# First product of a hybrid attention layer: tokens stationary and not turned, weights held for two sweeps, another order in the last unit, rotation tables made between the rows of x

## The reference

```python
h = rmsnorm(x, norm_w)
qa, ka, va, ga, qb, kb, vb, gb = split(h @ w_in)      # 8 differential heads; 16 q heads on 2 kv heads
qa, ka, qb, kb = rope(rmsnorm(each))                  # cos and sin of position * inv_freq
oa = sum over the causal keys of (softmax(qa0 ka0) - lam * softmax(qa1 ka1)) * va, in 128-query blocks
ob = softmax([band of 256 keys, sink]) @ vb           # window 128
y  = [rmsnorm(oa) * subln_w * (1 - lam_init) * silu(ga), ob * silu(gb)]      # (1024, 2048)
out = x + y @ w_out
```

## Time and profile before

| what | us |
|---|---|
| median of 3 runs | 1784.22 (1783.39 to 1784.88) |
| the profiled execution's own time | 1783.47 |
| its span, first to last instruction | 1781.7 |
| PE busy | 1745.5 (98%) |
| PEld busy | 1470.9 (83%) |
| DVE busy | 1190.4 (67%) |
| ACT busy | 813.5 (46%) |
| POOL busy | 450.0 (25%) |
| mean granted TensorE clock | 0.997 of full |

### The profile page before, as it was taken

How to read it: one execution, slowest core, us unless ns; L and a number is a source line. 1 busy time by engine, 2 the same in 40 slices (tenths; PEclk the granted TensorE clock), 3 DMA queues, 4 the chain that set the end, 5 groups by cost and what they waited for, 6 DMA issues and landing times.

```text
span 1781.7 us, 28435 instructions
## 1 busy us (share of the span) xinstructions
PE 1745.5 (98%) x8904; PEld 1470.9 (83%) x8904; DVE 1190.4 (67%) x2409; ACT 813.5 (46%) x2154; POOL 450.0 (25%) x668
## 2 busy tenths in 40 slices
PE   6999999999999999999999999999999988999999
PEld 6978888888888888888888888888888867778887
DVE  6742675866757767677676675876868788436764
ACT  5411445544544545454454544444544565333321
POOL 3231221412313223132131222422424334100000
PEclk9999999999999999999999999999999999999999
DMA  6222333433433333433334334453433666587665
GB/s 236 67 77 83 114 116 123 123 113 94 133 122 99 122 106 122 128 104 101 120 123 131 104 105 127 140 162 112 140 101 109 193 209 194 175 274 238 212 197 171
DMA packets 278091, 245.82 MB, mean 138 GB/s; under 512 B 32112, under 2 KB 220528, under 8 KB 276848
## 3 DMA queue, kind: packets, MB, share of 16 engines
q1 hardware_dynamic: 278000, 244.68, 43.8%
HBM read 174.35 MB, written 70.25 MB: 137 GB/s over the span
## 4 chain that ended last, share of the span: by engine, by line
PE 89%; DVE 3%; ACT 1%; DMA 0%; issue 0%; SPq 0%; DVEq 0%; ACTq 0%
PE ps_a L1048 22%; PE ps_a L1050 22%; PE ps_a L1049 22%; PE ps_b L1139 3%; PE ps_a L1099 3%; PE ps_b L1154 3%; PE ps_a L1098 2%; PE ps_b L1048 2%; PE ps_b L1049 2%; PE ps_b L1050 2%; PE ps_b L1092 2%; PE ps_b L1185 1%; PE ps_b L1156 1%; DVE w_lo_sb L1347 1%; PE ps_b L1168 1%; PE ps_b L1167 1%
## 5 line engine op out<-in xcount | busy, mean ns | idle before, releaser
L1048 PE MATMUL ps_a<-hT_hi,w_hi_sb 128*128 128x512 f32 x1600 | 651.8, 407 | 6.2 <-DVE w_lo_sb L1347 3.2
L1050 PE MATMUL ps_a<-hT_hi,w_lo_sb 128*128 128x512 f32 x1600 | 627.1, 392 | 0.0
L1049 PE MATMUL ps_a<-hT_lo,w_hi_sb 128*128 128x512 f32 x1600 | 624.3, 390 | 0.0
L1050 PEld LDWEIGHTS ps_a<-hT_hi,w_lo_sb 128*128 128x128 f32 x1600 | 300.5, 188 | 66.9
L1048 PEld LDWEIGHTS ps_a<-hT_hi,w_hi_sb 128*128 128x128 f32 x1600 | 301.1, 188 | 65.9 <-DVE w_lo_sb L1347 6.9
L1049 PEld LDWEIGHTS ps_a<-hT_lo,w_hi_sb 128*128 128x128 f32 x1600 | 301.9, 189 | 54.7
L1347 DVE TENSOR_TENSOR w_lo_sb<-w_raw_sb,w_hi_sb 128x512 fp32r<-128x512 f32 x305 | 230.2, 756 | 172.9 <-ACT w_hi_sb L819 171.3
L819 ACT ACTIVATE w_hi_sb<-w_raw_sb 128x512 fp32r<-128x512 f32 x304 | 189.9, 626 | 189.8 <-PE ps_a L1050 52.8
L1347 DVE TENSOR_TENSOR ps_a<-ps_a,mask 128x128 f32<-128x128 f32 (+2 forms) x192 | 77.8, 419 | 200.6 <-PE ps_a L1099 200.0
L937 ACT ACTIVATE attention_parts<-ps_b 128x512 fp32r<-128x512 f32 (+3 forms) x160 | 76.9, 521 | 213.3 <-PE ps_b L1139 213.2
L1018 ACT ACTIVATE expd<-ps_a,neg_max 128x256 f32<-128x256 f32 (+7 forms) x128 | 95.1, 743 | 158.3 <-DVE neg_max L1577 155.8
(11 more groups left out here) (147 smaller groups left out, 2840.3 us busy)
## 6 DMA issues: line engine op xcount, KB each, us to landing
w_raw_sb<-in_w_in SPq DMA_DIRECT2D x192, 256.0 KB, 3.0
w_out_sums<-in_w_out SPq DMA_DIRECT2D x64, 256.0 KB, 3.9
w_out_sums_dram<-w_out_sums SPq DMA_DIRECT2D x64, 256.0 KB, 2.8
w_raw_sb<-w_out_sums_dram SPq DMA_DIRECT2D x64, 256.0 KB, 3.0
qkv_a_dram<-stage_rows SPq DMA_DIRECT2D x48, 256.0 KB, 2.5
qkv_sb<-qkv_a_dram SPq DMA_DIRECT2D x64, 192.0 KB, 2.9
w_out_sums<-y_dram SPq DMA_DIRECT2D x24, 512.0 KB, 4.9
w_raw_sb<-in_w_out SPq DMA_DIRECT2D x48, 256.0 KB, 3.7
```

The lines of the kernel that those rows point to most:

```text
L1048: pe.matmul(dst, a_hi, b_hi, start=start, stop=False)
L1049: pe.matmul(dst, a_hi, b_lo, start=False, stop=False)
L1050: return pe.matmul(dst, a_lo, b_hi, start=False, stop=stop)
```

## The change

The first product now has the tokens of A11 stationary (128 of them at a time) and 512 columns of w_out moving, so that the result comes out with tokens on the partitions, and is stored from `stage` without turning. A tile is 256 tokens by 512 columns; tiles 0 and 1 use the same weights (n = 0), 2 and 3 the others. The weights of rows 0 to 511 stay in the ring's four buffers for both tiles (R0 to R3, then R4 to R7); those of rows 512 to 1023 are held in the place of hT that is free by then (`held`), loaded from a copy in DRAM that SP makes in the units of A, 64 rows in each. The ring's count before the output tiles is 8, not 16. In the last unit ScalarE evacuates ahead of its splits and does `second_b` behind `hi_qk`; VectorE does `lo_probs` between mask and maxima, and `y_out` behind `lo_qk`. The tables are made in pieces behind rows 1 to 6, ScalarE's sines behind row 6, and the small parameters are loaded between rows 2 and 3 of x. The semaphores for it, an added wait of S2's second half, and the counts of bank uses (without the two turns of the last stage) are left out here.

```diff
@@ -85,7 +85,12 @@
-NQ_OUT = NQ_IN + 16
+NQ_OUT = NQ_IN + 8
+RING_LOADS = {3: (4, 5), 6: (6,), 7: (7,)}
+RING_SPLITS = {0: (3,), 5: (4,), 6: (5,), 7: (6,), 8: (7,), 14: (8,), 15: (9,)}
+HELD_LOADS = {0: 0, 8: 1}
+HELD_SPLITS = {1: (0, 1), 2: (2, 3), 9: (4, 5), 10: (6, 7)}
@@ -404,6 +409,10 @@
+        def held(a, g):
+            return a[:, KT - 4 + g % 4, 512:1024]
@@ -444,13 +453,24 @@
-            def load_quarter_o(p, q):
-                Q = NQ_IN + 4 * p + q
+            def load_ring(R):
+                Q, n, kk = NQ_IN + R, R // 4, R % 4
                 wait(sp, sm["w_lo_ready"], Q - 1)
-                src = w_out[0, q * 2 * P:(q + 1) * 2 * P, p * 256:(p + 1) * 256].rearrange("(k r) c -> r k c", k=2)
-                sp.dma_start(w_raw[:, Q % 2, :].rearrange("p (k c) -> p k c", k=2), src)\
+                sp.dma_start(w_raw[:, Q % 2, :], w_out[0, kk * P:(kk + 1) * P, n * 512:(n + 1) * 512])\
                   .then_inc(w_in_sem[Q % 2], 16)
+            def load_held(n):
+                if n:
+                    sp.wait_ge(sm["p1_summed"], 2)
+                else:
+                    sp.wait_ge(sm["w_used"], NQ_IN)
+                    sp.wait_ge(sm["w_copied"], 16 * AH)
+                for c in range(2):
+                    r, k = (4 + 2 * c) * P, KT - 4 + 2 * c
+                    src = scr_w[r - 512:r - 512 + 2 * P, n * 512:(n + 1) * 512].rearrange("(k p) t -> p k t", p=P)
+                    sp.dma_start(hT_lo[:, k:k + 2, 512:1024].bitcast(F32), src).then_inc(p1w_in[c], 16)
@@ -550,17 +573,23 @@
+                if first == len(KINDS) - 1:
+                    if s in HELD_LOADS:
+                        load_held(HELD_LOADS[s])
+                    for R in RING_LOADS.get(s, ()):
+                        load_ring(R)
+                    if s >= 12:
+                        load_w_out(s - 12)
+                    return
...
-                    load_quarter_o(p, q)
+                    load_ring(q)
...
-                elif first == len(KINDS) - 1:
-                    load_w_out(q)
@@ -574,6 +603,13 @@
+                elif d["kind"] == "O":
+                    wait(sp, pp_copied[b], d["T"] + 1)
+                    n, r = d["p"] // 2, 2 * (d["p"] % 2) + b
+                    sp.dma_start(scr_part[r * P:(r + 1) * P, n * 512:(n + 1) * 512], stage[:, b, :])\
+                      .then_inc(stored[b], 16)
+                    return
...
@@ -652,7 +685,7 @@
-            for r in range(1, NR):
+            for r in range(1, 3):
@@ -667,6 +700,8 @@
+            for r in range(3, NR):
+                load_x(r)
@@ -690,9 +725,12 @@
-                    if d and s % 4 == 3 and not d["turned"]:
+                    if d and s % 4 == 3 and d["kind"] != "O" and not d["turned"]:
                         store_gate(d, 0)
                         store_gate(d, 1)
+                    if before["kind"] == "O" and (s == 0 or d and s % 4 == 0):
+                        for b in range(2):
+                            store_rows(before, b, None)
@@ -718,6 +756,9 @@
+                        if s == 4:
+                            sp.dma_start(scr_w[bass.ds(it * 64, 64), :], w_out[0, bass.ds(it * 64 + 512, 64), 0:1024])\
+                              .then_inc(sm["w_copied"], 16)
@@ -855,22 +896,24 @@
+                if r == 6:
+                    act.wait_ge(sm["rope_arg"], 2)
+                    act.activation(cos_t[:, :, :], cos_t[:, :, :], ACT.Sin).then_inc(sm["rope_ready"], 1)
+                    act.activation(sin_t[:, :, :], sin_t[:, :, :], ACT.Sin).then_inc(sm["rope_ready"], 1)
             kv_out(0)
+            act.wait_ge(sm["lam_sum"], 1)
+            act.activation(neg_lam[:, 2:4], neg_lam[:, 0:2], ACT.Exp).then_inc(sm["lam_exp"], 1)
...
+                elif before["kind"] == "O":
+                    wait(act, stored[b], (before["T"] + 1) * 16)
@@ -880,13 +923,20 @@
-                    wait(act, sm["w_used" if b else "pp_done"], u * 4 + 4 if b else u - 1)
+                    if b and d["kind"] == "O":
+                        act.wait_ge(sm["p1_summed"], d["p"] + 1)
+                    else:
+                        wait(act, sm["w_used" if b else "pp_done"], u * 4 + 4 if b else u - 1)
                     stage_free(before, b, it, first)
-                    if d["turned"]:
+                    if d["turned"] or d["kind"] == "O":
...
+            def held_high(g):
+                act.wait_ge(p1w_in[g % 4 // 2], 16 * (g // 4 + 1))
+                act.activation(held(hT_hi, g), held(hT_lo, g).bitcast(F32), ACT.Copy).then_inc(sm["p1w_hi"], 1)
@@ -902,14 +952,24 @@
-                    if d:
+                    last = first == len(KINDS) - 1
+                    if last and s % 4 == 3:
+                        evacuate(d, before, u, it, first)
+                    if last:
+                        for R in RING_SPLITS.get(s, ()):
+                            split_w(NQ_IN + R, R % 4)
+                        for g in HELD_SPLITS.get(s, ()):
+                            held_high(g)
+                    elif d:
                         split_w(Q0 + (s + 2), (s + 2) % 4)
+                        if first == len(KINDS) - 2 and s == 15:
+                            split_w(NQ_IN + 2, 2)
...
-                        if s % 4 == 3:
+                        if s % 4 == 3 and not last:
@@ -946,7 +1006,7 @@
-                        elif back1 and d:
+                        elif back1 and d and not last:
@@ -955,6 +1015,8 @@
+                        if back1 and last:
+                            second_b(back1)
@@ -1056,30 +1118,43 @@
-                if b == 0:
+                if b == 0 and not part_o:
...
-                    elif before["turned"]:
+                    elif before["turned"] or before["kind"] == "O":
...
+                    n, second = d["p"] // 2, d["p"] % 2
+                    t = slice((2 * second + b) * P, (2 * second + b + 1) * P)
+                    for kk in (2 * q, 2 * q + 1):
+                        if kk < 4:
+                            b_hi, b_lo = w_hi[:, kk, :], w_lo[:, kk, :]
+                            if b == 0 and not second:
+                                pe.wait_ge(sm["w_lo_ready"], NQ_IN + 4 * n + kk + 1)
+                        else:
+                            b_hi, b_lo = held(hT_hi, kk), held(hT_lo, kk)
+                            if b == 0 and not second:
+                                pe.wait_ge(sm["p1w_lo"], 4 * n + kk - 4 + 1)
                         if d["p"] == 0 and b == 0:
-                            wait(pe, sm["a11_lo"], kk + 1)
-                        mm = three(p_proj[b], w_hi[:, q, w], w_lo[:, q, w], operand(hT_hi, "A11", kk), operand(hT_lo, "A11", kk),
+                            pe.wait_ge(sm["a11_lo"], kk + 1)
+                        mm = three(p_proj[b], operand(hT_hi, "A11", kk)[:, t], operand(hT_lo, "A11", kk)[:, t], b_hi, b_lo,
                                    kk == 0, kk == HALF_K - 1)
...
+                    if q == 3:
+                        mm.then_inc(sm["p1_summed" if b else "pp_done"], 1)
+                    elif b and second and q < 2:
+                        mm.then_inc(sm["w_used"], 2)
+                    return
...
@@ -1237,7 +1312,6 @@
-                            turn_tile(tb[0], 0, use_number(tb[1], it, first), bank_of(tb[1], first))
@@ -1245,7 +1319,6 @@
-                            turn_tile(tb[0], 1, use_number(tb[1], it, first), bank_of(tb[1], first))
@@ -1373,6 +1446,46 @@
+            def angles():
+                dve.wait_ge(sm["pos_in"], 32)
...
+            def rope_reduce(table, quarter_turn):
...
+            def rope_finish(table, quarter_turn):
...
+            def lambda_sums():
+                dve.wait_ge(sm["lam_in"], 64)
...
@@ -1382,6 +1495,18 @@
+                if r == 1:
+                    angles()
+                elif r == 2:
+                    rope_reduce(cos_t, 0.25)
+                elif r == 3:
+                    rope_finish(cos_t, 0.25)
+                elif r == 4:
+                    rope_reduce(sin_t, 0.0)
+                elif r == 5:
+                    rope_finish(sin_t, 0.0)
+                elif r == 6:
+                    lambda_sums()
@@ -1577,14 +1671,17 @@
-            def max_b(st, j):
+            def mask_b(st):
                 lo = P if st["i"] == 0 else 0
-                gb = st["G"] - AH * NR
...
+            def max_b(st, j):
+                lo = P if st["i"] == 0 else 0
+                gb = st["G"] - AH * NR
@@ -1598,6 +1695,12 @@
+            def held_low(g):
+                dve.wait_ge(sm["p1w_hi"], g + 1)
+                tt(held(hT_lo, g), held(hT_lo, g).bitcast(F32), held(hT_hi, g).bitcast(F32), ALU.subtract)\
+                    .then_inc(sm["p1w_lo"], 1)
@@ -1681,8 +1784,16 @@
-                    if d:
+                    last = first == len(KINDS) - 1
+                    if last:
+                        for R in RING_SPLITS.get(s, ()):
+                            split_w(NQ_IN + R, R % 4)
```

(15 more changed lines are left out.)

89 lines of the change are left out of this document (39 added, 50 removed).

## The result

The kernel after takes 1786.76 us (median of 20 runs, 1783.78 to 1789.61), the kernel before 1783.58 us in the same sessions (20 runs): 1.0016 of it, 95% interval 1.0009 to 1.0023. It is slower by some 3 us. The forecast was 1784.0 us, a move of -0.3 us.

A forecast was written before the change was run, and what follows sets the result against it. TensorE is busy 98% of the span; the last unit is bound by a block-by-block loop through the other engines. -3.2 + 5.1 - 2.2 = -0.3 us on the profiled 1783.47 us, median 0.75 above: 1784.0 us, range 1775 to 1789.

The forecast's parts named there:

- The start, forecast -3.2 us: TensorE's wait at 90 us for a VectorE weight split goes once the tables move between x's rows: -3.2 us.
- x's row 3: At the start, row 3 lands at 28 to 31 us behind small loads, costing 0; late-row rival 1787 us, chance 0.07.
- The loop, forecast +5.1 us to the first output tile: Last unit's block loop: first output tile waits for block 7's exponentials, 1515.1 us instead of 1510.01: +5.1 us.
- where 11.5 to 12.5 was said: Expected sign in the last unit: 11.5 to 12.5 us from scores to scores in blocks 3 to 5.
- The last piece, from block 7's q/k to the tile: Block 7 adds y_out, a split, mask, probabilities, maxima and exponentials before the first output tile: 8.4 us.
- A fall inside the unit is mostly covered by y_out and the splits before the mask: Step on TensorE's clock in the last unit: falls to half clock add 0 us to the forecast sum.
- a sign of being wrong: The forecast is wrong if the granted clock shows several new stretches at half, or scores follow in 10 us or less throughout.
- The rival of the clock: TensorE idles 3 to 3.7 us in blocks 1, 3, 4, 5, some 3 us before the first output tile; three falls, +4.5.
- splits at 0.65 us each: Last unit's loop: six VectorE weight splits before a mask, 0.65 us each without GpSimd beside, 3.9 us in all.
- Behind the unit, forecast -2.2 us: Behind the first output tile, two turns (0.7 us) and a 1.45 us wait for copied turned rows go: -2.2 us.
- my bare loop of 9.9 us: Last unit, one block in the new order, before adding splits, evacuations and high parts: 9.9 us.
- the order works as meant: Rival: low parts of probabilities do not delay the maxima and 4.9 us of waits before scores go: 1772 us, chance 0.20.

The follow-up runs named there:

- tables_only: The kernel before with only the change's edits at the start (small loads behind x's row 2, tables in pieces): 1778.9 us, 0.9972 of before.
- maxima_first: The kernel after with VectorE's maxima put back straight behind the mask in the last unit, low parts of the probabilities behind them: 1776.9 us, 0.9966 of before.
- unit_only: The kernel after with the start of the kernel before, so only the last unit changed: 1790.9 us, 1.0037 of before.
- keep_clock: The kernel after with nine extra unread matmuls ahead of the first product's quarter in five steps of the last unit: 1783.4 us, 0.9999 of before.
- evac_early: The kernel after with ScalarE's evacuation of the finished tile moved ahead of the even step's exponentials: 1780.2 us, 0.9980 of before.
- orders_only: The kernel before with the change's start and its four last-unit orders, but the old product: 1787.1 us, 1.0022 of before.
- evac_clock: The kernel after with the edits of evac_early and keep_clock together: 1779.5 us, 0.9982 of before.
- evac_max: The kernel after with the edits of evac_early and maxima_first together: 1775.9 us, 0.9959 of before.
- before_orders: The kernel after with all four order edits of the last unit undone, the new product kept: 1778.5 us, 0.9971 of before.

## Why the prediction missed

**The start, forecast -3.2 us: -4.6.** The wait at 90 us went as worked out, and nothing came late behind it. x's row 3 behaved as said too: ScalarE's timeline of after has its square at 29.47 us, inside my 28 to 31,

```profile
29.47 1.91 ACT L872 ACTIVATE hT_lo<-x_raw_sb 128x2048 fp32r<-128x2048 f32 x1 [4.69 <-DMA x_raw_sb<-in_x]
```

and the scaling hides it. The Trainium skill (DMA: Bandwidth & Descriptors, "Rules for kernel authors") made the small loads the thing to watch; they held row 3 back by some 5 us, and none of it reached the end. The other 1.4 us I did not foresee, and the interval of tables_only does not tell them from none. The block-0 scores of before came at 1424.46 us and those of eleven of the twelve profiles with the new start at 1419.9 to 1420.7. The twelfth, maxima_first, had them at 1421.18 us, 3.3 before those of before, and it is the one that had as much half-clock time around 20 us as before had. Part of the rest may be that the wait had a second price. In the profile of unit_only, which keeps the wait, the clock falls behind it:

```profile
88.00:96.00 8.00, 4.94 (x15) 4.00 (x16) 3.54 (x7) 0.00 (x0) 4.21 (x5) 0.79 0.41 111
```

In the profile of before it did not the earlier trace rows. The rest is not accounted for: the half-clock time around 20 us varied between profiles, from none to 6.8 us, whatever the code.

**The loop, forecast +5.1 us to the first output tile: +8.2 by itself** (unit start to first tile, 97.15 us in after and 88.92 in before). The mechanism was named rightly: low parts between mask and maxima, `y_out` in front of the next mask, the evacuation and the splits on the chain. From scores to scores, blocks 3 to 5 took 13.3, 13.6 and 13.4 us where 11.5 to 12.5 was said, and block 6 9.6, near the 10 that was said; by the ends of the q/k low parts it is 12.7, 12.3, 13.5 and 11.4. The last piece, from block 7's q/k to the tile, was 8.44 us, as forecast (8.4). The step that failed is the one that took no fall of the clock into the loop, "A fall inside the unit is mostly covered by y_out and the splits before the mask"; the sum held 0 us for it, and keep_clock, which kept the clock up, measured 3.4 us. Five came, which the prediction had named as a sign of being wrong, and scores behind a slow quarter were late for the mask, by 1.2 us in block 6:

```profile
1496.40 1.30 DVE L1420 TENSOR_TENSOR ps_a<-ps_a,mask 128x512 f32<-128x512 f32 x2 [1.17 <-PE ps_a L1174]
```

With the clock kept up, block 6 is 9.8 us from end to end of the q/k low parts, as said. The rival of the clock (three falls, +4.5 against the measured +3.2) had the mechanism. Where it was thin is the place of the falls. It had one at the first output tile. This profile of after has none there, but that is chance: of the six profiles that have the wait of 2.48 or 2.49 us before that tile, four (unit_only, keep_clock, evac_early, orders_only) show the clock at half from within 1.3 us of the tile's start, and two (after, evac_clock) do not. A fall lasts 3.4 us, or twice that, by the granted clock; the 3.8 that the prediction read from slices is too long. The Trainium skill (TensorE: Matmul & The Clock Gate, "Part 1: The HAM clock gate") has the slow clock as the default that activity lifts; the trace agrees in that each of the five falls came with an idle stretch. The prediction's reading of it, that each new idle stretch may cost a fall, holds for five of six in this profile.

A smaller term was mis-sized as well: splits at 0.65 us each. VectorE's timeline, the same instruction twice:

```profile
1477.24 1.29 DVE L1420 TENSOR_TENSOR hT_lo<-hT_lo,hT_hi 128x512 fp32r<-128x512 f32 x2 [2.61 <-ACT hT_hi L939]
...
1481.70 2.86 DVE L1420 TENSOR_TENSOR hT_lo<-hT_lo,hT_hi 128x512 fp32r<-128x512 f32 x2
```

and GpSimd's beside the second:

```profile
1481.03 2.98 POOL L1952 TENSOR_TENSOR hT_lo<-hT_lo,hT_hi 128x512 fp32r<-128x512 f32 x2
```

Two held low parts took 2.86 us beside GpSimd's low parts and 1.29 us without them: 1.6 us on the chain of block 5, ahead of a mask. In the profile the loop took 8.2 - 5.1 = 3.1 us more than forecast; keep_clock's loop is 2.3 us shorter, and these low parts could be the rest; no run takes them apart.

**Behind the unit, forecast -2.2 us: -1.5** (from the first output tile to the end 271.7 us before, 270.1 after). One pair of profiles does not measure this term: the same piece took 269.5 us in tables_only, whose code there is that of before, and 268.0 to 273.2 us in the other profiles with the new product.

By the profiles: -4.6 + 8.2 - 1.5 = +2.1 us, which is the difference of the spans. I had -0.3: the start that came out better (by 1.4 us) hides a part of the loop's miss (3.1 us).

**What the working did not ask.** It priced the change's order and never compared it with the old order under the new product. The two prices were there: my bare loop of 9.9 us, and the old one, which by the same rows is 11.4 less a split, a high part of S3, an evacuation and one more split, 8.3. That is 1.6 us for each block, in the direction of the 8.2 us of orders_only. It is too much in size: in the profiles the six blocks 1 to 6 of orders_only took 5.4 us longer than those of tables_only, 0.9 each, and from block 7's q/k to the tile another 2.1. The rival "the order works as meant" (1772 us) was wrong about this order; a kernel near its time came only by turning it round.

## What to carry to other kernels

Where a loop runs through several engines, put between two of its links only what the next link needs; work that feeds the next block goes beside the longest step of another engine. Price each edit of an order against the order it replaces, with everything else as new, since a good edit (the start, -4.6 us) and a neutral one (the product) can be hidden by a bad one. And a wait of TensorE that looks free costs again in the matmuls behind it if the clock falls: count an idle stretch together with what stands behind it.

## What the runs showed of the hardware

- TensorE's clock fell to half five times in after's unit, the first time behind an idle stretch of 2.19 us, but not behind 2.48 us before the first output tile, and in before not behind 3.2 us, where in unit_only the same wait ended in a fall. Other profiles have falls behind shorter waits: 1.83 us in maxima_first, 1.85 in evac_max, 1.97 in before_orders. TensorE's timeline of after has its shortest that led to a fall and the one that led to none, and that of evac_early (last line) has the same wait as the latter with a fall, its first matmul 0.80 us instead of 0.50:

```profile
1428.53 0.50 PE L1110 MATMUL ps_a<-hT_hi 128*128 128x512 f32 x1 [2.19 <-DVE hT_lo L1420]
...
1513.67 0.50 PE L1110 MATMUL ps_a<-w_hi_sb,hT_hi 128*128 128x512 f32 x1 [2.48 <-ACT expd L1091]
...
1508.91 0.80 PE L1110 MATMUL ps_a<-w_hi_sb,hT_hi 128*128 128x512 f32 x1 [2.48 <-ACT expd L1091]
```

- What a fall costs depends on what is behind it: 8.5 us of lost clock became 3.4 in keep_clock and the time fell by 3.4 us; with the evacuation off the chain 8.5 became 0.0 and the time fell by 0.7 us.
- A VectorE subtraction with both inputs in SBUF took 1.4 us instead of 0.65 beside GpSimd's of the same kind, while one that reads PSUM (0.68 us at 1480.31, beside GpSimd's scaling of the probabilities) kept its time. A VectorE instruction of 128x4 took 1.15 instead of 0.16 us beside one of GpSimd's of 1.3 us. The Trainium skill (GPSIMD Engine Reference, "1. Specifications") says that the two engines share SBUF interfaces and contend where VectorE has two SBUF inputs; the trace agrees for the subtractions, with the factor 2.2 (2.86 against 1.29 us for two).
